# Modulation chunks multiplied in one visit of four instead of visits of one and two

## The chip, the cores and the metric
The kernel runs on one core of a Trainium2 chip. The metric is device time in microseconds of one execution; lower is better. PE is TensorE, PEld its weight loads, DVE is VectorE, ACT is ScalarE, POOL is GpSimd, SP is SyncE, which here issues the loads of weights.

## What is computed
Two model blocks one after the other on a sequence of 256 tokens of 2048 features, all in float32. The change lies in the first part of the first block: the modulation vector (one product of a 12288-column matrix, for two inputs `c` and `c_ctx`) and the input projection of `x` and of `ctx`.

```python
def adaln(cvec, w, b):
    m = jax.nn.silu(cvec) @ w + b
    return jnp.split(m[:, None, :], N_MOD, axis=-1)
...
        sh1, sc1, ga1, sh2, sc2, ga2 = adaln(c, w_mod[i], b_mod[i])
        csh1, csc1, cga1, csh2, csc2, cga2 = adaln(c_ctx[None, :], w_mod[i], b_mod[i])
        px = modulate(rms_norm(x, norm_mix[i]), sh1, sc1) @ w_in[i]
        pc = modulate(rms_norm(xc, norm_mix[i]), csh1, csc1) @ w_in[i]
...
        x = x + ga1 * yx
        x = x + ga2 * ffn(modulate(rms_norm(x, norm_ffn[i]), sh2, sc2),
                          w_gate[i], w_up[i], w_down[i])
```

`sh1` and `sc1` are needed for the projection. The other four parts (`ga1`, `sh2`, `sc2`, `ga2`) are needed much later, so their columns of `w_mod` are multiplied on the side, between the chunks of the projection.

## The kernel before
All weights stream from HBM in chunks of 512 rows by 256 columns (512 KB, `CK` = 4 blocks of 128 rows, `CN` = 256). A chunk is one DMA of SP into a buffer. `STREAM` (line 52) lists the phases in order: `mod` (shift and scale), then `in_kv`, `in_lora`, `in_r`, `in_rest` (the projection), `out`, `ffn` and so on. A phase has trips (loops), a trip has pairs (256 columns of output each, two PSUM banks), and a pair has four main chunks of rows, here called M0 to M3.

A **main chunk** is split into two parts, since a product of float32 precision is made from several faster ones: ACT copies its high part (`hi`, line 898), DVE subtracts to get the rest (`lo`, line 1330), and PE multiplies. `hi` and `lo` have four slots (`RING`); in `in_kv` and `in_lora` main chunks use only two of them, as the other two hold modulation chunks. In `in_kv` and the first pair of `in_lora` PE makes three products per block (lines 2127 to 2129, for `x` and `ctx`), in the second pair of `in_lora`, in `in_r` and in `in_rest` two (lines 2117 and 2118, `x` alone).

A **modulation chunk** (side chunk; `whole` in the code) is multiplied as it is, in `mod_rows` (line 2154): four matmuls of 32 columns of weights, each into its own quarter of a PSUM bank. Four modulation chunks make one side row of 256 columns. When the fourth is done, DVE copies the row out of PSUM (`mod_row2`, line 1464); PE turns it into columns with two small matmuls (`side_columns`, line 2220), which waits for that copy through `side_free` and stands behind the chunk that follows the row's last one; later DVE adds the bias (`mod_bias`, line 1469).

What fixes the order is `Phase.order`, written out in lines 72 to 81: a list of (side or main, pair or side row, rows) over one trip. Every engine walks this same list, in its own program order. With `SIDES` side rows a trip, two pairs a trip and four modulation chunks a row, `in_kv` and `in_lora` put two modulation chunks ahead of each main chunk, `in_r` and `in_rest` one. Trips and pairs: `in_kv` 4 trips of 2 pairs, `in_lora` 1 of 2, `in_r` 2 of 2, `in_rest` 4 of 2.

- **SP** (line 757) issues the loads in the order of the list; before each it waits for its buffer. A main chunk's buffer is free when its last content is split, a modulation chunk's when PE has used it; the first ones of the later buffers wait for a whole region, as `side_proj` does for the finished operand of the first layer (`region_free`, line 625).
- **ACT** (line 900) and **DVE** (line 1333): at entry j they first split all main chunks up to j + lookahead, then do the side work of this entry (`side`, such as the operand groups of `GROUP_AT` in `in_kv`, or the convolution and small vectors in `in_rest`), and then the evacuation of a pair or the copy of a side row that j completes. A split of `hi` waits until PE has used its slot before.
- **PE** (line 2081): at entry j it waits for the split or the load, multiplies, and then runs `after`, here the columns.

The lookahead (line 327) is 4 in `in_kv` and `in_lora`, 6 in `in_r` and `in_rest`.

The evacuation of a pair is on DVE: in `in_kv` four shifted multiply-adds on 128x510 (lines 1475 and 1477) behind two copies of ACT; in `in_r` ACT's copy (919), DVE's sum (1359), ACT's scaled copies (1020) and DVE's four multiply-adds; in `in_rest` ACT's copy and DVE's sum alone. In the third and fourth trip of `in_rest`, `conv`, `conv_gate` and `lam_powers` on DVE and `conv_and_rates` on ACT run behind certain entries of the list.

Of the kernel before, what the change touches and what calls it, by code (L numbers as in the profile page):

```python
# [63 lines left out]
class Phase:  # L64


    def __init__(self, name, trips, pairs, rows, g0, p0):
        self.name, self.trips, self.pairs, self.rows = name, trips, pairs, rows
        self.per_pair = n = rows // CK
        self.g0, self.p0 = g0, p0  # L70

        self.order = []
        if name == "out_2":
            self.order = [(False, p, c) for c in range(n) for p in range(pairs)]
        self.rows_order = (0, 2, 3, 1) if name == "out" else range(n)
        if name == "out":
            self.order = [(False, p, c) for cs in ((0, 2, 3), (1,)) for p in range(pairs) for c in cs]
        for p in range(pairs if name not in ("out", "out_2") else 0):
            for c in self.rows_order:
                per = SIDES.get(name, 0) // pairs  # L80
                self.order += [(True, per * p + t // n, t % n) for t in range(per * c, per * c + per)] + [(False, p, c)]
        self.chunks = len(self.order)

    def chunk(self, i, j):
# [165 lines left out]
def program(nc, A, out):  # L250
# [6 lines left out]
    def at(name, offset, shape, dt=F32):  # L257
        return nc.alloc_sbuf_tensor_at(name, shape, dt, offset=base + offset)
# [7 lines left out]
    mod = at("mod", fix + 2048, [P, 2, 6 * KB])  # L266
# [57 lines left out]
    bank_free, tmp_ready = sem("bank_free"), sem("tmp_ready")  # L324
    SPLIT_CREDIT, BANK_CREDIT = RING, 2
    EARLY = {"mod", "in_kv", "in_lora", "in_r", "in_rest"}
    lookahead = lambda ph: 2 if ph.name == "mod" else 4 if ph.name in ("in_kv", "in_lora") else 6 if ph.name in EARLY else 3
    SPLIT_EARLY = [PH["out"].chunk(0, 2), PH["out"].chunk(0, 3), PH["out"].chunk(0, 4), PH["out"].chunk(0, 5), PH["ffn"].chunk(0, 3)]
    TURN = (1, 3, 4, 6)
    VEC_AT = 5  # L330
# [2240 lines left out]
```

How the kernel before makes its waits and increments, by code:

```python
    def wait(self, eng, name, rounds=0):  # L146
        eng.wait_ge(self.sem, self.value(name, rounds))
# [13 lines left out]
    def wait(self, value):  # L161
        self.eng.wait_ge(self.sem, value)
# [536 lines left out]
    def load_vectors(eng, which):  # L699
        eng.wait_ge(vec_clear, 1)
        for number, (name, (t, first, n)) in enumerate(VROWS.items()):
            if number % 2 != which:
                continue
            if name.startswith("shift"):
                c0, width = {"shift_rkv": (0, P), "shift_gd": (GD0, P), "shift_wd": (WD0, LORA),
                             "shift_ad": (WD0 + LORA, LORA)}[name]
                src = A["rw_shift"][:, c0:c0 + n // 3 * width]
                for tap in range(3):
                    eng.dma_start(vrow[first + tap * (n // 3):first + (tap + 1) * (n // 3), t, 0:width],
                                  src[tap].rearrange("(n c) -> n c", c=width)).then_inc(vec_in[which], 16)
                continue
            src = A[name]
            names = " ".join("abcd"[:len(src.shape)])
            flat = src.rearrange(f"{names} -> ({names})") if len(src.shape) > 1 else src
            eng.dma_start(vrow[first:first + n, t, :], flat.rearrange("(n c) -> n c", c=P)).then_inc(vec_in[which], 16)
# [43 lines left out]
                def trip(i):  # L760
# [5 lines left out]
                            load_vectors(sp, 0)  # L766
                        if chunks[ph.chunk(i, j)].raw_free:
                            sp.wait_ge(*chunks[ph.chunk(i, j)].raw_free)
                        dst, arrives, _ = raw_at(ph, i, j)
```

## Time and profile before
| | |
|---|---|
| Median of three executions | 3071.35 us (3059.32 to 3072.09) |
| The profiled execution | 3060.31 us, span 3058.4 us |
| PE busy | 2976.7 us, 97% of the span |
| DVE busy | 1861.4 us, 61% |
| ACT busy | 1386.1 us, 45% |
| Mean granted clock of TensorE | 0.988 of full |
| Chain that ended last | PE 86%, DVE 8%, DMA 3% |

The phases that the change touches run from about 116 to 564 us. The page cuts the span in 40 slices and gives the busy share of each engine in tenths; in the slices from 153 to 562 us PE has a 9 in each. The busy time of PE counts matmuls that overlap, so a full share says that it had no hole, not that it worked at its peak; the timelines show by their start times what a step costs. A timeline row is: start, duration, engine, line, operation, output and inputs, shape, count of records merged, and in brackets the idle time before it with who ended it. A float32 matmul of `mod_rows` leaves two records.

### The profile page before, as it was taken

What the parts mean: (1) busy time and instruction counts of PE and PEld (TensorE: products, weight loads), DVE (VectorE), ACT (ScalarE), POOL (GpSimd) and SP (SyncE); (2) the same over time, 40 slices, a digit from 0 to 9 for tenths busy, and PEclk for the clock granted to TensorE, in tenths of its full rate; (3) what the DMA queues carried; (4) which work ended last, traced back from release to release, by engine and by line L of the source; (5) the groups of instructions that cost most, each with busy time, mean ns of one, the idle gap of its engine ahead of it and who ended that gap; (6) DMA issues with size and microseconds to landing.
All of it is one profiled execution on the core that took longest, in us unless ns stands there. A gap on an engine that the chain in (4) does not pass through costs nothing.

```text
span 3058.4 us, 62116 instructions
## 1 busy us (share of the span) xinstructions
PE 2976.7 (97%) x26987; PEld 2522.6 (82%) x26987; DVE 1861.4 (61%) x2655; ACT 1386.1 (45%) x1985; POOL 242.0 (8%) x299
## 2 busy tenths in 40 slices
PE   5899999999999999999999999999999999999998
PEld 2677777889888887888888888888888888888887
DVE  1333354677788776555555555789976666665554
ACT  1411233565665444444444444456644444444433
POOL 1000000143332200000000000012200000000000
PEclk7999999999999999999999999999999999999999
DMA  9997799200000065655666555655556666656664
GB/s 339 289 287 228 250 314 297 80 8 8 8 12 8 19 221 156 186 183 185 192 185 186 186 186 186 213 171 162 162 165 191 188 189 189 188 189 196 189 190 144
DMA packets 549240, 529.54 MB, mean 173 GB/s; under 512 B 16916, under 2 KB 545706, under 8 KB 548074
## 3 DMA queue, kind: packets, MB, share of 16 engines
q1 hardware_dynamic: 546074, 516.08, 54.0%
q0 software_dynamic: 2832, 9.49, 0.9%
q8 instruction: 214, 3.51, 0.5%
q14 instruction: 56, 0.46, 0.0%
q10 hardware_dynamic: 64, 0.02, 0.0%
HBM read 521.32 MB, written 4.19 MB: 172 GB/s over the span
## 4 chain that ended last, share of the span: by engine, by line
PE 86%; DVE 8%; DMA 3%; issue 1%; SPq 1%; ACT 1%; DVEq 0%; ACTq 0%
PE ps L2117 41%; PE ps L2118 20%; PE ps L2254 10%; PE ps L2158 2%; PE ps L2127 2%; DVE lo L1330 2%; PE ps L2128 2%; PE ps L2129 2%; DMA raw_more<-in_w_mod 1%; PE ps L2277 1%; PE ps L2264 1%; PE ps L2510 1%; PE ps L2262 1%; DVE dirs L1740 1%; SPq L773 1%
## 5 line engine op out<-in xcount | busy, mean ns | idle before, releaser
L1330 DVE TENSOR_TENSOR lo<-raw,hi 128x1024 fp32r<-128x1024 f32 x776 | 947.6, 1237 | 710.5 <-ACT hi L898 707.7
L2117 PE MATMUL ps<-mov,hi 128*128 128x512 f32 x3680 | 1299.3, 398 | 4.9 <-DVE mov L1393 4.1
L898 ACT ACTIVATE hi<-raw 128x1024 fp32r<-128x1024 f32 x776 | 810.7, 1056 | 864.8 <-PE ps L2118 652.3
L2118 PE MATMUL ps<-mov,lo 128*128 128x256 f32 x3680 | 1027.4, 279 | 0.0
L2117 PEld LDWEIGHTS ps<-mov,hi 128*128 128x128 f32 x3680 | 691.7, 188 | 191.6 <-issue 27.1
L2118 PEld LDWEIGHTS ps<-mov,lo 128*128 128x128 f32 x3680 | 694.0, 189 | 0.1
L2117 PE MATMUL ps<-hid,hi 128*128 128x512 f32 x704 | 248.8, 399 | 0.0
L919 ACT ACTIVATE tmp<-ps 128x512 f32<-128x512 f32 x157 | 93.8, 598 | 254.4 <-PE ps L2118 247.0
L2118 PE MATMUL ps<-hid,lo 128*128 128x256 f32 x704 | 197.7, 281 | 0.0
L2510 PE MATMUL ps<-mov,hi 128*128 128x512 f32 x512 | 187.1, 408 | 0.0
L812 POOL TENSOR_TENSOR lev<-U,kscan 128x256 f32<-128x256 f32 x192 | 152.1, 828 | 236.7 <-ACT U L1126 236.7
L2117 PEld LDWEIGHTS ps<-hid,hi 128*128 128x128 f32 x704 | 132.3, 188 | 33.2
L2117 PE MATMUL ps<-hid_2a,hi 128*128 128x512 f32 x448 | 155.7, 394 | 0.0
L2511 PE MATMUL ps<-mov,lo 128*128 128x256 f32 x512 | 142.7, 279 | 0.0
L2118 PEld LDWEIGHTS ps<-hid,lo 128*128 128x128 f32 x704 | 133.0, 189 | 0.0
L2118 PE MATMUL ps<-hid_2a,lo 128*128 128x256 f32 x448 | 124.1, 277 | 0.0
L2127 PE MATMUL ps<-mov,hi 128*128 128x512 f32 (+1 forms) x288 | 118.0, 410 | 2.9 <-DVE lo L1330 2.9
L2510 PEld LDWEIGHTS ps<-mov,hi 128*128 128x128 f32 x512 | 96.1, 188 | 23.1 <-DVE lo L1330 1.4
L2128 PE MATMUL ps<-mov,hi 128*128 128x512 f32 (+1 forms) x288 | 114.2, 396 | 0.0
L2129 PE MATMUL ps<-mov,lo 128*128 128x512 f32 (+1 forms) x288 | 113.3, 394 | 0.0
L2117 PEld LDWEIGHTS ps<-hid_2a,hi 128*128 128x128 f32 x448 | 84.0, 188 | 19.5
L2254 PE MATMUL ps<-dirs,lev 64*64 64x64 f32 x2560 | 91.7, 220 | 8.2 <-DVE dirs L1740 3.3
(387 smaller groups left out, 3841.4 us busy)
## 6 DMA issues: line engine op xcount, KB each, us to landing
raw<-in_w_in SPq DMA_DIRECT2D x184, 512.0 KB, 4.7
raw<-in_w_gate SPq DMA_DIRECT2D x88, 512.0 KB, 4.5
raw<-in_w_up SPq DMA_DIRECT2D x88, 512.0 KB, 4.5
raw<-in_w_down SPq DMA_DIRECT2D x88, 512.0 KB, 4.4
raw<-in_w_ffn_gate SPq DMA_DIRECT2D x88, 512.0 KB, 4.5
raw<-in_w_ffn_up SPq DMA_DIRECT2D x88, 512.0 KB, 4.6
raw<-in_w_ffn_down SPq DMA_DIRECT2D x88, 512.0 KB, 4.4
raw<-in_w_out SPq DMA_DIRECT2D x64, 512.0 KB, 4.5
```

The source lines that it names most:

```text
L812: scan_pool[d].done(pool.tensor_tensor(LEV[l][d][:, :, :], U[d][:, :, :], over_chunks(level[1 - d][l]), ALU.mult), (q, f"m{l}"))
L898: act.activation(hi[:, s, :, :], src, ACT.Copy).then_inc(hi_ready, 1)
L919: act.activation(tmp[:, t, :, :], ps[:, b:b + 2, T:2 * T], ACT.Copy).then_inc(tmp_ready, 1)
L1330: dve.tensor_tensor(lo[:, s, :, :], raw_at(ph, i, j)[0], hi[:, s, :, :].bitcast(F32), ALU.subtract)\
L2117: pe.matmul(ps[:, b, :], hi[:, s, kk, w], moving(k, None), start=first, stop=False)
L2118: mm = pe.matmul(ps[:, b, 0:T], lo[:, s, kk, w], moving(k, 0), start=False, stop=last)
L2127: pe.matmul(ps[0:widths, b, :], hi[:, s, kk, w], mov1[:, k, 0, :, :], start=first, stop=False)
L2128: pe.matmul(ps[0:widths, b, :], hi[:, s, kk, w], mov1[:, k, 1, :, :], start=False, stop=False)
L2129: mm = pe.matmul(ps[0:widths, b, :], lo[:, s, kk, w], mov1[:, k, 0, :, :], start=False, stop=last)
L2254: mm = pe.matmul(ps[hs, 4 * d + bank, off + c * n:off + (c + 1) * n], lhs(c, hs), moving, start=True, stop=True)
L2510: pe.matmul(ps[:, b, :], w_hi[:, kk, :], on_mov(k, None), start=(k == 0), stop=False)
L2511: mm = pe.matmul(ps[:, b, 0:T], w_lo[:, kk, :], on_mov(k, 0), start=False, stop=(k == KB - 1))
```

## The change
The list puts all four modulation chunks of a side row together, ahead of the main chunk where the row began: in `in_kv` and `in_lora` four ahead of M0 and four ahead of M2 of each pair, in `in_r` and `in_rest` four ahead of M0. The number of chunks and what is multiplied stay the same. The lookahead becomes 5 in all four phases (and stays 2 in `mod`, 3 in the later ones).

```diff
@@ -78,7 +78,8 @@
         for p in range(pairs if name not in ("out", "out_2") else 0):
             for c in self.rows_order:
                 per = SIDES.get(name, 0) // pairs
-                self.order += [(True, per * p + t // n, t % n) for t in range(per * c, per * c + per)] + [(False, p, c)]
+                side = c * per // n if per and c * per % n == 0 else None
+                self.order += [(True, per * p + side, t) for t in range(n) if side is not None] + [(False, p, c)]
         self.chunks = len(self.order)
 
     def chunk(self, i, j):
@@ -324,7 +325,7 @@
     bank_free, tmp_ready = sem("bank_free"), sem("tmp_ready")
     SPLIT_CREDIT, BANK_CREDIT = RING, 2
     EARLY = {"mod", "in_kv", "in_lora", "in_r", "in_rest"}
-    lookahead = lambda ph: 2 if ph.name == "mod" else 4 if ph.name in ("in_kv", "in_lora") else 6 if ph.name in EARLY else 3
+    lookahead = lambda ph: 2 if ph.name == "mod" else 5 if ph.name in EARLY else 3
```

One trip of `in_rest` (s a modulation chunk, M a main one; two pairs) is s M s M s M s M twice before, and ssss MMMM twice after. One pair of `in_kv` is ss M ss M ss M ss M before, and ssss M M ssss M M after.

## Rows read from the trace of the kernel before
**Rows 1.** Windows: the stretch of `in_r`, busy time, clock, DMA, GB/s.
```profile
core 0: us, PE busy (x) PEld busy (x) DVE busy (x) ACT busy (x) POOL busy (x), PEclk, DMA share, GB/s
372.00:462.00 90.00, 90.00 (x639) 67.07 (x637) 50.45 (x69) 35.39 (x43) 0.56 (x1) 1.00 0.98 311
```
**Rows 2.** Waits of PE from 130 to 600 us: total, times, longest.
```profile
PE ps L2254 <- ACT XY L1136: 1.0, 1, 1.0
```
**Rows 3.** Timeline of PE in `in_rest`, around one visit of one chunk.
```profile
461.89 0.50 PE L2220 MATMUL ps<-basics,mrow 128*128 128x2 f32 x4
...
465.70 0.28 PE L2118 MATMUL ps<-mov,lo 128*128 128x256 f32 x1
465.91 0.64 PE L2158 MATMUL ps<-side_ctx,c 128*32 128x256 f32 x8
466.48 0.50 PE L2117 MATMUL ps<-mov,hi 128*128 128x512 f32 x1
466.81 0.28 PE L2118 MATMUL ps<-mov,lo 128*128 128x256 f32 x1
466.93 0.40 PE L2117 MATMUL ps<-mov,hi 128*128 128x512 f32 x1
...
469.45 0.42 PE L2158 MATMUL ps<-side_ctx,c 128*32 128x256 f32 x4
```
**Rows 4.** Timeline of PE in `in_kv`: a main chunk and a visit of two.
```profile
167.05 0.50 PE L2127 MATMUL ps<-mov,hi 128*128 128x512 f32 x1
...
172.76 1.07 PE L2158 MATMUL ps<-side_r,c 128*32 128x256 f32 x16
173.76 0.50 PE L2127 MATMUL ps<-mov,hi 128*128 128x512 f32 x1
```
**Rows 5.** Timeline of PE in `in_r`: what follows a pair's last chunk.
```profile
403.46 0.50 PE L2220 MATMUL ps<-basics,mrow 128*128 128x2 f32 x4
```
**Rows 6.** Timeline of DVE in `in_r`, behind that pair's evacuation.
```profile
407.71 2.36 DVE L1330 TENSOR_TENSOR lo<-raw,hi 128x1024 fp32r<-128x1024 f32 x2
...
415.33 0.43 DVE L1464 COPY mrow<-ps 128x256 f32<-128x256 f32 x1 [1.75 <-PE ps L2158]
```
**Rows 7.** Timeline of DVE in `in_rest`: the first split behind an evacuation.
```profile
463.67 1.23 DVE L1330 TENSOR_TENSOR lo<-raw,hi 128x1024 fp32r<-128x1024 f32 x1 [0.26 <-ACT hi L898]
```
**Rows 8.** Timeline of DVE, third trip of `in_rest`: side work.
```profile
508.63 1.22 DVE L1546 TENSOR_TENSOR proj<-proj 128x1024 f32<-128x1024 f32 x1
...
519.27 0.47 DVE L1475 SCALAR_TENSOR_TENSOR ymix<-proj,vec,ymix 128x252 f32<-128x252 f32 x1
```
**Rows 9.** Timelines of ACT and DVE, fourth trip of `in_rest`: side work.
```profile
536.57 0.20 ACT L1030 ACTIVATE lcol<-vec 128x8 f32<-128x8 f32 x1
...
538.20 0.62 ACT L1033 ACTIVATE wdad<-wdad 96x512 f32<-96x512 f32 x1
...
541.41 0.17 DVE L1526 TENSOR_SCALAR lcol<-vec 128x8 f32<-128x8 f32 x1
...
542.13 0.42 DVE L1558 TENSOR_TENSOR ymix<-ymix,proj 128x256 f32<-128x256 f32 x1
```
**Rows 10.** Timeline of all engines in `in_lora`: pair's end, first split behind it.
```profile
372.04 0.50 PE L2220 MATMUL ps<-basics,mrow 128*128 128x2 f32 x4
...
375.96 1.21 DVE L1330 TENSOR_TENSOR lo<-raw,hi 128x1024 fp32r<-128x1024 f32 x1
```
**Rows 11.** Timelines of DVE, ACT and PE at the start of `in_kv`.
```profile
141.59 0.48 DVE L1450 SCALAR_TENSOR_TENSOR mov<-xhat_last,mod,mov 128x256 fp32r<-128x256 f32 x1
...
149.01 1.06 ACT L898 ACTIVATE hi<-raw 128x1024 fp32r<-128x1024 f32 x1 [8.18 <-DMA raw<-in_w_in]
...
153.32 0.50 PE L2127 MATMUL ps<-mov,hi 128*128 128x512 f32 x1
```
**Rows 12.** PE: a long wait in the timeline; windows of PE with the clock.
```profile
2214.94 0.55 PE L2481 MATMUL ps<-kret,p 128*128 128x128 f32 x1 [2.73 <-DVE p L2023]
...
1156.00:1166.00 10.00, 5.86 (x18) 0.51 0.03 12
...
2214.00:2221.00 7.00, 6.06 (x17) 0.52 0.43 141
```

## Prediction
> **What bounds the kernel now.** I read the granted clock and the busy shares by stretch first, then what PE waited for, then the timelines of PE, DVE and ACT around one modulation visit. In the stretch that the change touches, PE is busy for all of the 90.00 us from 372 to 462 at full clock, DVE for 50.45 and ACT for 35.39 [rows 1]; and from 130 to 600 us the longest wait of PE for anyone is 1.0 us [rows 2]. So PE sets the time there, DVE is behind it with slack, and two things count: what PE spends on visits, and whether the slack of DVE survives a new order. The sum is made against the profiled execution, 3060.31 us (span 3058.4), which lies 11 us below the median of 3071.35.
>
> **What goes: visits.** PE passes 88 times from main chunks to modulation chunks and back: `in_kv` 32 times, `in_lora` 8, `in_r` 16, `in_rest` 32. After it, 16, 4, 4 and 8, so 32; 56 visits go, no chunk does. A visit of one chunk: the last main matmul starts at 465.70, the next main one at 466.48, so 0.78; without a visit it is 0.12 (466.81 to 466.93), and the first main pair is longer by 0.10 after it (466.48 to 466.81 is 0.33, usually 0.23), so 0.76 [rows 3]. The eight records of one chunk take 0.57 to the next main matmul, the sixteen of two chunks 1.00 [rows 3, 4]: a chunk more costs 0.43. What is left, 0.76 - 0.43 = 0.33 us, is the price of the visit. 56 x 0.33 = **18.5 us gained**, all on the path. Bounds: 0, if a visit of four has a cost in it that I don't see (none is in the trace), and 0.45 a visit, 25 us.
>
> **What moves: the copy that PE waits for.** Line 1464 on DVE takes the finished side row out of PSUM; PE's next step on it, the columns of line 2220, stands one chunk later in PE's order, and PE works in order: all main chunks are queued behind it. Before, the modulation chunk that completes a row comes last in a pair, and that chunk and the main one behind it cover the copy. Now all four chunks come first, the columns are due right after the first main chunk M0, and DVE has in its order, between the end of the pair before and this copy: the evacuation of that pair, the splits of M1, M2 and M3 (with a lookahead of 5 they are called at j = 0, 1 and 2 of the pair, the copy at j = 3), any side work, then the copy. Let T be where PE begins what follows the last main chunk.
>
> PE after T: a visit of four, 0.57 + 3 x 0.43 = 1.86; then M0, 466.48 to 469.45 less the 0.09 by which the next visit starts later, 2.9. Columns are due at T + 4.8 in `in_r` and `in_rest` [rows 3].
>
> *After a pair of `in_r` or the second of `in_lora`*, T is 403.46 [rows 5]. DVE begins its first split behind the evacuation at 407.71, two of them take 2.36, so three 3.5, the copy 0.43 [rows 6]: done at 411.65, seen at 411.7, due at 408.3. **Gap 3.4 us**, five times (four pairs of `in_r`, the first of `in_rest`): 17.0.
>
> *After a pair of `in_rest`*, T is 461.89 [rows 3]; the first split starts at 463.67 [rows 7], copy done at 467.6, due at 466.7. **Gap 1.0**, three times: 3.0.
>
> *The last four pairs* carry side work ahead of the copy. Third trip: a product of 1.22 in the first pair, two blocks of two taps of 0.5 in the second [rows 8]: gaps 2.2 and 3.1. Fourth trip, first pair: ACT puts 2.25 us (536.57 to 538.82, a table load in it) between the hi parts of M2 and M3, and DVE a gate of 0.42 and 0.7 of small operations (541.41 to 542.13) [rows 9]: hi of M3 ends 6.0 after T, split 7.2, gate and small ones 8.3, copy 8.8, gap 4.0. Second pair: another such load, and the lookahead now reaches the first chunk of `out`, whose split (1.2) comes ahead of the copy: gap 4.3 likewise. Together 13.6.
>
> *`in_kv`* has longer main chunks, 5.7 from 167.05 to the next visit at 172.76 [rows 4]: due at T + 7.5, while DVE is through the evacuation at T + 3.9 and done with one split and the copy by T + 5.6 [rows 10]. No gap; the 1.9 us left are the cover. *`in_lora`*, second pair, short chunks: the same DVE work against T + 4.8: gap 0.8.
>
> Gaps: 17.0 + 3.0 + 13.6 + 0.8 = **34.4 us lost**. Bounds: 20, if one split fewer stood ahead of each copy than I order (five gaps of 2.2, the short ones none, 8.9 of the last four); 38, with semaphore and restart times of 0.3 more each.
>
> **The start of `in_kv`.** SP keeps its order: four modulation chunks now stand ahead of M0 and again ahead of M4. Today the operand of the first layer is ready at 142.07, which frees the buffers of the next modulation chunks; M4 is the third load behind that and lands by 149.01, its split is done at 151.3, PE needs it at 153.32: slack 2.0 [rows 11]. After it M0 lands two loads later (0.52 MB at the 311 GB/s of [rows 1] is 1.7 us each; the queue was not always full there, so I take 1.45), M1 ends near 139.7, and the call for M3's hi, which needs M1's end, moves from j = 7 to j = 6, ahead of the last two groups of the operand: hi until 140.8, then two times four steps of about 0.45 on ACT with DVE behind each, ready near 145.9, 3.9 us later. M4 is the fifth load, 2.9 later. 3.9 + 2.9 - 2.0 = **4.8 us lost** (bounds 1 and 8: the loads may overlap more, the start may be slower). Before M4 PE stands for 3.3 us, as the four modulation chunks ahead of it land in time to be done near 154.9. Further loads have more lead than now: with gaps a pair of `in_r` takes 17 us for the same eight chunks, and its DMA share of 0.98 [rows 1] falls.
>
> **The clock.** Where PE stood for 2.73 us, after a stretch at full clock, the granted clock was 0.52 over the next 7 us (2214 to 2221), the lower of its two levels, 1.2 of 2.4 GHz [rows 12]. Of such a time some 5.5 us are work behind a gap of 3.4, at half the clock: at most 2.75 lost, 2.5 taken. Nine gaps are of 2.7 us or more (the start, five, three of the last four): 9 x 2.5 = **22.5 us lost**. Bounds: nothing, and 3.9 each if the clock stays low for 10 us, as from 1156 to 1166 [rows 12].
>
> The Trainium skill, "TensorE: Matmul & The Clock Gate", section "HAM oscillation — how this bites in real kernels", says that a wait in every tile of a loop lets the clock fall in every tile, and gives a rule of thumb from what length on idle gaps hurt. The 2.73 us here lie under that length and the clock fell all the same, so the trace does not agree and I go by it; by the rule only the two gaps of over 4 us would pay, 5 us in place of 22.5, and the sum would be 3097.
>
> **Sum.** -18.5 + 34.4 + 4.8 + 22.5 = +43.2: 3060.3 + 43.2 = 3103.5 on the profiled execution, and 3071.35 + 43.2 = 3114.5 on the median, which I predict.
>
> **The rivals.**
> *The clock holds* through gaps of 3 to 4 us between bursts of 13 us: -18.5 + 34.4 + 4.8 = +20.7, so 3092 on the median (3081 on the profiled level). For it: the fall is seen behind one gap that stands alone. Against: the other low stretch, at 0.51, stands behind waits for DVE too [rows 12], and [rows 2] has no wait above 1.0 us that the clock outlived.
> *Gaps about half as long*, if a split stands elsewhere than I order it: 17 us of gaps, only the start and the table loads slow the clock (7.5 less 2.5 for a shorter start): -18.5 + 17 + 4.8 + 5 = +8, 3079. Against it: DVE's order is fixed in the program.
> *Faster*: the copy comes in time, because something shortens the DVE queue between T and M0's end from 8.2 us to 4.8; then only the visits count, -18.5, 3053. It decides at a copy done by T + 4.8; today's rows put its earliest finish there at T + 5.7, behind the short evacuation.
> *The change doesn't do what it says*: a visit of four costs as much as two of two. Then 18.5 more, 3133.
>
> **How the numbers follow.** Forecast with gaps and clock 0.55, clock holds 0.18, half gaps 0.13, faster 0.10, no saving 0.04. The forecast's own range is 3097 to 3134 (gaps 28 to 38, clock 1.5 to 3.5 each). Down to 3076 the range takes in the clock holding on either level of the median and the upper part of the half gaps; what is left out is the faster case, the low part of the half gaps and a tail above. Range 3076 to 3134. 0.5% is 15 us, about what can be told from no change here. Slower by more than that: 0.55 + 0.04 + 0.17 = 0.76; faster 0.10 with a few of its runs within 15 us, so 0.09; the rest, 0.15, within.
>
> **What would show it.** In the profile after: PE waits for DVE's copy of L1464 at the columns, some twelve times, 3.4 us after `in_r`; sixteen or thirty-two records of L2158 in a row; 56 fewer stretches in which a weight load of a main chunk waits for issue; a granted clock of half in several places between 380 and 600 us; a wait for M4's split near 155. Wrong it would be if PE's busy time stays closed from 372 to 564, or if the copy stands ahead of the splits.

## The result and the profile after
The kernel after takes 3109.93 us (median of four runs, 3088.86 to 3115.49) against 3065.34 for the kernel before (3059.12 to 3072.09) run beside it. The medians lie 44.6 us apart, the means of the four runs each 40.6 us, which is a ratio of 1.0132, with a 95% interval of 1.0077 to 1.0188. So the change makes the kernel slower, by some 40 to 45 us; a median of 3114.5 was predicted, with a range of 3076 to 3134. The profiled execution took 3111.11 us, span 3109.2, at a mean granted clock of 0.981.

From the edit of the list on, lines of the kernel after are one further down than before (L1465 is the copy, L2221 the columns, L2159 the modulation matmuls, L2118 and L2119 the products of `x` alone, L1331 `lo`).

Waits of PE in the kernel after, 110 to 620 us (total, times, longest), to be held against [rows 2]:
```profile
PE ps L2221 <- DVE mrow L1465: 30.8, 13, 4.0
PE ps L2128 <- DVE lo L1331: 3.3, 1, 3.3
```
Before, no wait of PE from 130 to 600 us was above 1.0 us. Now PE stands thirteen times at the columns for DVE's copy of the side row, and once for M4's split. Both kernels have one more wait ahead of 130 us, in front of M0 of `in_kv`: 2.9 us before, 2.8 after. Ahead of that lie waits for loads, of 1.5 us at most before and 1.9 after.

Where one of them comes from, in the first pair of `in_r`, behind the evacuation of `in_lora`: timelines of PE, then of DVE, in the kernel after:
```profile
398.11 0.61 PE L2221 MATMUL ps<-basics,mrow 128*128 128x2 f32 x4 [3.15 <-DVE mrow L1465]
...
393.64 0.48 DVE L1478 SCALAR_TENSOR_TENSOR gd<-px,vec,gd 128x255 f32<-128x255 f32 x1
...
394.24 3.49 DVE L1331 TENSOR_TENSOR lo<-raw,hi 128x1024 fp32r<-128x1024 f32 x3
397.64 0.42 DVE L1465 COPY mrow<-ps 128x256 f32<-128x256 f32 x1
```
DVE goes without a pause from the evacuation through the bias (0.16 us, left out here) and three splits (3.49 us) to the copy; it ends at 398.06 and PE starts at 398.11. The row itself was complete at 391.87, where PE began M0 behind the visit. The copy is late by its place in DVE's list.

Windows of the kernel after (PE busy, clock, DMA share, GB/s; the first also with PEld, DVE, ACT and POOL behind PE). The first answers to [rows 1]; the others lie behind six of the waits:
```profile
372.00:462.00 90.00, 76.81 (x526) 60.52 (x525) 39.32 (x56) 26.68 (x34) 0.56 (x1) 0.92 0.80 257
...
398.00:406.00 8.00, 7.89 (x37) 0.79 1.06 350
416.00:424.00 8.00, 7.25 (x25) 0.57 1.06 345
455.00:463.00 8.00, 7.39 (x43) 1.00 1.06 352
472.00:480.00 8.00, 7.17 (x43) 1.00 1.06 348
532.00:537.00 5.00, 4.52 (x18) 0.66 0.92 285
549.00:557.00 8.00, 6.28 (x21) 0.57 1.04 335
```
In the first stretch PE is busy for 76.81 us of 90 where it was busy for all of them; DVE's work fell from 50.45 to 39.32, as less of the program fits in the window (526 records of PE in place of 639). The clock is at half for a part of the time behind the waits at 398.11 and 416.75 (3.15 and 3.19 us in the timeline), but not behind those at 455.61 and 472.83, which are as long, 3.15 us each.

**Where the time went.** The starts of PE's first matmul of a phase or trip give a table by stretch. M0 is the first main chunk of a phase or trip; the columns run from M0 to M0, the last one from M0 to the last main matmul of `in_rest`. All numbers are in us, from one profile of each kernel; the experiments in it are told below.

| kernel | M0 of `in_kv` to M0 of `in_r` | `in_r` | `in_rest`, trips 1 and 2 | trip 3 | trip 4 |
|---|---|---|---|---|---|
| before | 266.84 | 58.48 | 58.42 | 29.22 | 28.09 |
| after | 267.60 | 74.73 | 60.80 | 36.93 | 38.90 |
| e_fill | 268.49 | 68.76 | 61.14 | 32.88 | 33.42 |
| e_la6 | 269.56 | 74.03 | 58.50 | 30.45 | 36.22 |
| e_late | 268.58 | 58.27 | 55.42 | 27.22 | 25.16 |
| e_late_groups | 262.33 | 58.03 | 55.76 | 27.23 | 25.15 |
| b_all | 262.45 | 55.31 | 54.45 | 27.23 | 26.05 |
| e_kv_clean | 267.08 | 58.44 | 58.43 | 29.21 | 28.10 |
| b_rest_clean | 268.05 | 54.98 | 54.45 | 27.23 | 25.99 |

After is 37.9 us longer than before over these five stretches; `in_r` gives 16.3 of it, the last two trips 18.5. The borders move a little with the order: one modulation chunk more lies in the first column of after (0.43) and three fewer in the last (1.3). From the first visit of `in_kv` (116.87 before, 114.90 after) to the first wait of the next phase (578.13, 616.93) the kernel after takes 40.8 us longer; this is the figure for the terms of the prediction to be held against.

The two profiled spans differ by 50.8 us. Some 13 us of that come after 2200 us, where the change touches nothing. One group of matmuls of the last stage, in the kernel before, then in the kernel after (form, count, busy us, mean ns of one, idle time before them):
```profile
L2117 PE MATMUL ps<-hid_2b,hi 128*128 128x512 f32 x256 | 89.1, 394 | 0.0
...
L2118 PE MATMUL ps<-hid_2b,hi 128*128 128x512 f32 x256 | 90.8, 399 | 0.0
```
The same matmuls, with no wait, go 1.9% slower in the one execution (90.8 for 89.1). It isn't the change's doing: among the kernels below, all with the same code there, the mean is 391, 394 or 399 ns, and `e_late`, `e_la6` and `e_fill`, which have the new order throughout, show 394 like the kernel before. The medians, which are over several executions, differ by 44.6.

### The profile page after: what moved, and what is told of

Read it like the earlier page. It is cut to its first block, busy times and chain, and to the rows that moved or that the text cites. A ratio compares the mean times of both kernels' runs of the same rounds, so it can differ in the third digit from the quotient of the medians.

```text
span 3109.2 us, 62114 instructions
## 1 busy us (share of the span) xinstructions
PE 2994.7 (96%) x26987; PEld 2547.5 (82%) x26987; DVE 1859.2 (60%) x2655; ACT 1382.0 (44%) x1985; POOL 241.9 (8%) x299
## 4 chain that ended last, share of the span: by engine, by line
PE 84%; DVE 10%; DMA 3%; ACT 2%; issue 1%; SPq 1%; DVEq 0%; ACTq 0%
PE ps L2118 40%; PE ps L2119 20%; PE ps L2255 10%; DVE lo L1331 4%; PE ps L2128 2%; PE ps L2129 2%; PE ps L2130 2%; DMA raw_more<-in_w_mod 2%; PE ps L2159 1%; PE ps L2278 1%; PE ps L2265 1%; PE ps L2511 1%; PE ps L2263 1%; DVE dirs L1741 1%; PE ps L2221 1%
## 5 line engine op out<-in xcount | busy, mean ns | idle before, releaser
L1331 DVE TENSOR_TENSOR lo<-raw,hi 128x1024 fp32r<-128x1024 f32 x776 | 946.4, 1237 | 700.3 <-ACT hi L899 698.1
L2118 PE MATMUL ps<-mov,hi 128*128 128x512 f32 x3680 | 1318.2, 403 | 4.8 <-DVE mov L1394 4.1
L2119 PE MATMUL ps<-mov,lo 128*128 128x256 f32 x3680 | 1038.9, 282 | 0.0
L2118 PEld LDWEIGHTS ps<-mov,hi 128*128 128x128 f32 x3680 | 699.9, 190 | 183.3 <-issue 6.2
L2119 PEld LDWEIGHTS ps<-mov,lo 128*128 128x128 f32 x3680 | 703.0, 191 | 0.1
L2118 PE MATMUL ps<-hid,hi 128*128 128x512 f32 x704 | 248.8, 399 | 0.0
L2119 PE MATMUL ps<-hid,lo 128*128 128x256 f32 x704 | 197.7, 281 | 0.0
L2511 PE MATMUL ps<-mov,hi 128*128 128x512 f32 x512 | 187.2, 408 | 0.0
L2118 PEld LDWEIGHTS ps<-hid,hi 128*128 128x128 f32 x704 | 132.3, 188 | 33.0
L2118 PE MATMUL ps<-hid_2a,hi 128*128 128x512 f32 x448 | 158.7, 399 | 0.0
L2119 PEld LDWEIGHTS ps<-hid,lo 128*128 128x128 f32 x704 | 133.0, 189 | 0.0
L2119 PE MATMUL ps<-hid_2a,lo 128*128 128x256 f32 x448 | 125.8, 281 | 0.0
L2511 PEld LDWEIGHTS ps<-mov,hi 128*128 128x128 f32 x512 | 96.1, 188 | 23.0 <-DVE lo L1331 1.2
L2118 PEld LDWEIGHTS ps<-hid_2a,hi 128*128 128x128 f32 x448 | 84.2, 188 | 21.0
```

What stands on the lines that cost most here:

```text
L1331: dve.tensor_tensor(lo[:, s, :, :], raw_at(ph, i, j)[0], hi[:, s, :, :].bitcast(F32), ALU.subtract)\
L2118: pe.matmul(ps[:, b, :], hi[:, s, kk, w], moving(k, None), start=first, stop=False)
L2119: mm = pe.matmul(ps[:, b, 0:T], lo[:, s, kk, w], moving(k, 0), start=False, stop=last)
L2511: pe.matmul(ps[:, b, :], w_hi[:, kk, :], on_mov(k, None), start=(k == 0), stop=False)
```

## The experiments
Each kernel is the one after with the edit shown; the ratio is to the kernel before, run on the same chip in the same job, with its 95% interval. The kernel before had medians of 3060.89, 3060.74 and 3061.55 us in the three jobs; a ratio takes in all runs of a job, so it can differ by some tenths of a per cent from that of the medians.

**Columns later (e_late).** If the copy costs time only because PE needs it so early, a later step of PE takes the cost away. In `in_r` and `in_rest` PE's columns go from one entry behind a row's last chunk to three; the order of DVE's work stays.
```diff
-                    done = ph.completed(j - 1) if j else None
+                    late = 3 if ph.name in ("in_r", "in_rest") else 1
+                    done = ph.completed(j - late) if j >= late else None
```


> The changed kernel, with one edit: in in_r and in_rest PE makes the columns of a side row three entries of the list after the row's last chunk (behind M2) instead of one (behind M0). DVE's order is untouched. My theory (PE stands because it reaches the columns before DVE's copy, which is queued behind three splits): the waits of PE for the copy go from 30.8 us to about 0.5 (the one of in_lora), in their place PE may wait some 0.6 us for M1's split in five pairs; the clock stays at full from 380 to 600; what is left is 18.5 us gained by visits against 3 to 5 us lost at the start of in_kv, so about 3052 to 3062, 0.2 to 0.4% below the kernel before. Rival (the visits of four themselves or the splits' place cost the time, the wait only shows it): the time stays near 3100, and the wait turns up at the splits instead.


Measured: 3053.51 us, 0.9974 (0.9946 to 1.0003). Waits of PE, 110 to 620 us:
```profile
PE ps L2128 <- DVE lo L1331: 3.3, 1, 3.3
PE ps L2118 <- DVE lo L1331: 2.7, 5, 0.6
```
The waits for the copy are gone but for one of 0.6, no low clock is left from 380 to 600 us (the window shows 1.00), and the five stretches take 434.7 where after takes 479.0. So the time lost lies in where PE waits for the copy and in what follows from that. What is left is five short waits for splits (0.5 to 0.6 us each, where the lookahead of 5 is now a little short) and the start of `in_kv`.

**A lookahead of 6 again (e_la6).** With the new order the lookahead decides what stands ahead of the copy. One entry more puts a split ahead of the evacuation in place of behind it.
```diff
-    lookahead = lambda ph: 2 if ph.name == "mod" else 5 if ph.name in EARLY else 3
+    lookahead = lambda ph: 2 if ph.name == "mod" else 5 if ph.name in ("in_kv", "in_lora") else 6 if ph.name in EARLY else 3
```
The last trip of `in_rest` keeps 5 (the loop over the lookahead is one shorter there).


> The changed kernel with the lookahead of in_r and in_rest back at 6, except in the last trip of in_rest, where it stays 5. So one split fewer stands ahead of each copy in DVE's queue. My theory: each of the five large gaps falls by one split, 3.15 to about 2.0 us, the three of 0.7 vanish, two of the last four fall by 1.2 and one by 0.9: waits of PE for the copy 30.8 to some 19 us, fewer falls of the clock, 3085 to 3100 in all. Rival (the lookahead of 5 is the whole cause and the new order costs nothing): the waits vanish and the time is below the kernel before, near 3050.


Measured: 3081.77 us, 1.0076 (1.0048 to 1.0105).
```profile
PE ps L2222 <- DVE mrow L1466: 20.8, 10, 3.9
```
The waits fall by 10.0 us, nearly as far as expected; the time lies a little below what was expected (3085 to 3100). The gaps do depend on the splits in the list, and the rival, in which the lookahead was the whole cause, falls: the time doesn't come down to 3050. But `in_r` hardly gains (74.73 to 74.03). Windows of PE from 380 to 470 us, in the kernel after, then in e_la6:
```profile
380.00:470.00 90.00, 77.05 (x528) 0.92 0.78 249
...
380.00:470.00 90.00, 80.26 (x530) 0.89 0.85 272
```
PE stands less there (five waits of 9.7 us in all, where after has four of 12.6), and the clock is low for longer. Three of the five are of 2.0 us now, and so is the next one behind them, at 475.51. Each of the four had half clock behind it: the windows from 421, 438 and 475, 6 us each, show 0.72, the one of 7 us from 456 shows 0.52. Shorter gaps didn't bring less of the low clock.

**The gaps filled (e_fill).** This separates the price of the clock from that of the gaps: ahead of its wait PE makes matmuls whose result nobody reads, about as many as fit in each gap.
```diff
+            def FILL(ph, i, m):
+                if ph.name == "in_r" or (ph.name, i, m) == ("in_rest", 0, 0):
+                    return 13
+                if ph.name == "in_rest":
+                    return (2, 2, 2, 2, 8, 11, 15, 17)[2 * i + m]
+                return 0
...
                         m = done[1]
+                        for n in range(FILL(ph, i, m)):
+                            pe.matmul(ps[:, 7, :], mov1[:, 0, 0, 1, 0:P], mov1[:, 0, :, 1, :], start=True, stop=True)
```


> The changed kernel, and PE multiplies something useless into a free bank ahead of each wait for the copy in in_r and in_rest: 13 matmuls of 512 columns at the large gaps (about 3.0 us), 2 at the small ones, 8 to 17 at the last four. Nothing else differs; the output doesn't use it. This tells the wait from the clock. My theory (a gap of about 3 us costs its own length and in more than half of the cases another 1.5 to 3 us of a clock at half): the waits for the copy fall to a few us in all, the time of the gaps stays, the granted clock is 1.00 from 380 to 600 us, and the time falls by 10 to 20 us against the changed kernel, to about 3090 to 3098. Rival (the clock costs nothing, as DVE and not PE sets the pace there): the time stays within 4 us of the changed kernel, 3106 to 3112.


Measured: 3084.63 us, 1.0072 (1.0043 to 1.0101). Windows of e_fill over two stretches of the kernel after that are shown above:
```profile
416.00:424.00 8.00, 7.78 (x46) 1.00 1.05 349
...
549.00:557.00 8.00, 8.00 (x68) 1.00 0.72 232
```
The useful work behind each gap starts no sooner after it than in the kernel after, and yet this is faster, by more than was expected (3090 to 3098): the clock is at 1.00 in both stretches, and over the whole of 380 to 600 us. Of the two ratios, 1.0072 here and 1.0132 for after, the intervals overlap, so it is the profile that shows the gain and not the times alone. From `in_r` on the table gives 196.2 us for 211.4, so 15.2 came back, and the clock is what differs. What after lost to the clock there is more than this, as the filling is a little longer than the gaps. The next section takes it from after itself.

**The two halves (e_kv_only, e_rest_only).** The new order in `in_kv` and `in_lora` alone, and in `in_r` and `in_rest` alone; the phases named in the edit keep the old list and the old lookahead.
```diff
+                if name in ("in_r", "in_rest"):
+                    self.order += [(True, per * p + t // n, t % n) for t in range(per * c, per * c + per)] + [(False, p, c)]
+                    continue
                 side = c * per // n if per and c * per % n == 0 else None
```


> The new order in in_kv and in_lora alone (lookahead 5 there); in_r and in_rest as before (order and lookahead 6). My theory: 20 visits go (-6.6 us), the start costs 3 to 5 us of waiting for M4's split and some 1.5 of low clock, in_lora 0.6: between -2 and +1 us against the kernel before, same; no wait of PE for the copy but 0.55 in in_lora. Rival (the start of in_kv carries much of the loss): 10 us or more slower than before.


Measured: 3066.97 us, 1.0031 (1.0005 to 1.0057).


> The new order in in_r and in_rest alone (lookahead 5 there); in_kv and in_lora as before (order and lookahead 4). My theory: 36 visits go (-11.9 us), the waits of PE for the copy stay, 30.2 us without that of in_lora, and the clock falls in several of them (10 to 17 us): 28 to 36 us slower than before, so nearly all of the changed kernel's loss. Rival (the loss is spread over all four phases): 10 to 20 us slower.


Measured: 3088.25 us, 1.0109 (1.0051 to 1.0167). The loss lies in `in_r` and `in_rest`, where the pairs are short; `in_kv` and `in_lora` have little of it. By the medians the second half is 27.5 us slower than the kernel before, just under the 28 to 36 that I expected. The first half came out worse than I expected, 6 us slower by the medians, and its timelines show why (DVE, then PE):
```profile
390.55 1.23 DVE L1334 TENSOR_TENSOR lo<-raw,hi 128x1024 fp32r<-128x1024 f32 x1 [3.65 <-ACT hi L902]
...
391.76 0.42 DVE L1468 COPY mrow<-ps 128x256 f32<-128x256 f32 x1
...
392.23 0.49 PE L2224 MATMUL ps<-basics,mrow 128*128 128x2 f32 x3 [2.87 <-DVE mrow L1468]
```
The lookahead of 5 in `in_lora` reaches over the end of the phase to the first main chunk of `in_r`, which there, with the old list, is only one chunk further. DVE waited 3.65 us for that chunk's `hi`, split it, and only then made the copy. That wait is of my edit, not of the change. The second half has one like it: with a lookahead of 4 in `in_lora`, `in_r`'s M0 is split behind the evacuation, and PE waits 3.3 us for it; it takes the place of the wait for the copy in that pair.

**The first half without that (e_kv_clean).** At two entries near the end of `in_lora`, 20 and 21 of 0 to 23, the lookahead stops short of `in_r`'s first main chunk:
```diff
-                        for n in range(1, lookahead(ph) + 1):
+                        for n in range(1, (24 - j if ph.name == "in_lora" and j in (20, 21) else lookahead(ph)) + 1):
```


> Visits of four in in_kv and in_lora alone, and the split of in_r's first main chunk kept behind the last copy of in_lora, so that the wait of 2.9 us of the run before it goes. Theory (a visit is worth 0.28 us, the start costs 5.7, the clock's fall near 157 us some 3): 20 visits x 0.28 = 5.6 gained, 5.7 + 0.7 + 3 lost, so about 4 us slower than before, ratio near 1.001, one wait for the copy of about 0.6 us and one for M4's split of 3.3. Rival (a visit is worth 0.33 and more and the start is hidden): 7 us faster, ratio 0.998.


Measured: 3062.41 us, 0.9996 (0.9972 to 1.0020); waits of PE:
```profile
PE ps L2131 <- DVE lo L1334: 3.3, 1, 3.3
...
PE ps L2224 <- DVE mrow L1468: 0.5, 1, 0.5
```
The waits are the two that were expected. The interval takes in both the theory's ratio (1.001) and the rival's (0.998), so the time doesn't tell them apart; the profile does. From the first visit of `in_kv` to M0 of `in_r` it takes 276.43 us (116.62 to 393.05) where the kernel before takes 272.94 (116.87 to 389.81), 3.5 longer, against some 4 of the theory. The 20 visits saved here don't quite pay for the start.

**The start of `in_kv` (e_late_groups).** e_late, with the last four groups of the operand made one or two entries earlier, so that the buffers come free earlier:
```diff
-    GROUP_AT = {0: 2, 1: 3, 3: 4, 4: 5, 6: 6, 7: 7}
+    GROUP_AT = {0: 2, 1: 3, 2: 4, 3: 5, 4: 6, 5: 7}
```


> The kernel with late columns, and the operand groups of the first layer called at j = 0 to 5 of in_kv instead of at 0, 1, 3, 4, 6 and 7, so that the last two stand ahead of M3's split. My theory of the start (M4's load is held up since the buffers ahead of it wait for the operand, which stands behind M3's split): the operand is ready near 137 instead of 145, the wait of PE for M4's split (3.3 us) vanishes with the fall of the clock behind it; 4 to 6 us less than with late columns alone. Rival (M4 is late because the queue of loads is full): the wait stays, no change.


Measured: 3050.97 us, 0.9961 (0.9929 to 0.9993). M4's wait is gone, and the first stretch takes 262.33 us for e_late's 268.58: 6.25 less, a little over what was expected. The medians, of two jobs, differ by 2.5 us only, and the intervals of the ratios overlap, so the times don't show this gain apart. PE in e_late, then in e_late_groups, in the windows and the timeline around M4:
```profile
154.00:168.00 14.00, 10.35 (x54) 0.76 1.10 351
...
155.45 1.93 PE L2159 MATMUL ps<-side_proj,c 128*32 128x256 f32 x32
157.31 0.50 PE L2128 MATMUL ps<-mov,hi 128*128 128x512 f32 x1
```
Of the 6.25 us 3.3 are the wait itself; the rest is the clock, which in e_late is at half for about half of the 14 us from 154 (0.76), and at 1.00 in that window in e_late_groups. The groups are all that was moved, so M4's wait came from the time at which the operand was finished, as the prediction put it. No run keeps a lookahead of 4 in `in_kv` with the new order, so how much of the start comes from the lookahead of 5 and how much from the list isn't shown.

**The faster version (b_all, b_rest_late, b_rest_clean).** b_all puts the three cures together: columns later, lookahead 6 in `in_r` and `in_rest`, groups earlier. b_rest_late leaves the old order in `in_kv` and `in_lora` and has columns later and lookahead 6. b_rest_clean is that with a lookahead of 5 at the last entry of `in_lora`.


> Late columns, lookahead 6 in in_r and in_rest, and the operand groups at j = 0 to 5, all with the new order in all four phases. My theory: no wait of PE for copy, split or load from 130 to 560 us but 0.6 in in_lora; only the 56 visits are left, so 15 to 19 us below the kernel before, ratio 0.994 to 0.995. Rival (something else in the new order costs PE time, or a visit costs less than 0.33 us): less than 10 us below.

> The new order in in_r and in_rest alone, with late columns and lookahead 6; in_kv and in_lora as before, with their old start. 36 visits go and no wait comes: my theory says 11 to 12 us below the kernel before, ratio 0.996. Rival (a visit costs half of what I read from the start times): 6 us below.

> Visits of four in in_r and in_rest alone, columns three entries later, lookahead 6 there, and the first main chunk of in_r split ahead of in_lora's evacuation. Theory: 36 visits x 0.28 = 10 us gained and nothing lost, since the wait of 3.3 us at 399 is gone and with it the fall of the clock behind it: ratio near 0.9967, from the first visit to the end of the projections 10 us less than before. Rival (the wait at 399 is not from the order of that split): it stays, and the ratio stays at 0.9986.


Measured: b_all 3035.57 us, 0.9942 (0.9915 to 0.9969); b_rest_late 3048.67, 0.9986 (0.9952 to 1.0020); b_rest_clean 3048.98 in a later job, 0.9954 (0.9927 to 0.9981). Waits of PE in b_rest_late for M0 of `in_r` and for the copy, then in b_rest_clean for M0:
```profile
PE ps L2121 <- DVE lo L1334: 3.3, 1, 3.3
...
PE ps L2225 <- DVE mrow L1468: 2.7, 2, 2.1
...
PE ps L2121 <- DVE lo L1334: 0.2, 1, 0.2
```
The wait for M0 went with the place of one split, as the theory had it and the rival not. It wasn't the only one in b_rest_late, which missed its expectation of no wait and 0.996: in `in_kv`, where this kernel has the old order, a load landed late (ACT stood 10.35 us for it, until 151.97; 8.18 us, until 149.01, in the kernel before), and PE waited 2.1 us for the copy that stands behind that chunk's split. From M0 of `in_kv` to M0 of `in_r` b_rest_late takes 275.05 us and b_rest_clean 268.05; the two waits and 3.4 us of half clock behind the first, which cost half of that, make up the 7.0. So the step from 0.9986 to 0.9954 is in part that load, and the two intervals overlap. b_all has two waits for the copy of 0.6 us and one for a split of 0.6 from 130 to 560 us, two more than expected. b_all and b_rest_clean are both faster than the kernel before, and by about what the visits are worth (b_all's ratio is 18 us, with 9.5 to 26 in its interval): the order of the change is good for about half a per cent once the copy has its time. b_all has the lowest median of all kernels here, though its interval overlaps those of b_rest_clean, e_late_groups and e_late.

## Why the prediction was right, point by point
**The visits.** Trip 3 of `in_rest` holds eight modulation chunks between its M0 and the next in both orders, and six visits fewer in the new one; without waits it takes 27.22 us in e_late (508.19 to 535.41) and 29.22 before:
```profile
506.71 0.50 PE L2117 MATMUL ps<-mov,hi 128*128 128x512 f32 x1
...
535.93 0.50 PE L2117 MATMUL ps<-mov,hi 128*128 128x512 f32 x1
```
2.0 / 6 = 0.33 us a visit, the predicted figure. A visit of four takes 1.87 in the kernel after (464.73 to 466.60), 1.86 predicted. In `in_kv`, between its first chunk and `in_lora`'s, 16 visits fewer give 4.7 us in e_late_groups, 0.29 each. So the 56 visits are worth 17 to 18 us, 18.5 predicted, and they were gained; the rival in which the change doesn't do what it says falls.

**The gaps at the copy.** Predicted 34.4 us, in thirteen places by the prediction's own list ("some twelve" in its last paragraph). Measured 30.8 in thirteen, and 0.16 more from each end of a wait to the pace of before (restart), about 33 in all. There are four of 3.15 to 3.19 in `in_r`'s pairs and one more of 3.15 in the first of `in_rest` (3.4 predicted), three of 0.66 to 0.73 in the next pairs (1.0); the last four are 2.03, 2.74, 3.55 and 3.98 (2.2, 3.1, 4.0, 4.3), and the one in `in_lora` is 0.55 (0.8). Each is 0.2 to 0.5 shorter than predicted. In the first pair of `in_r`, with T at 390.01, the copy ended 8.05 us after T and not 8.2, and PE's M0 ended 4.96 after it and not 4.8. The rival of gaps half as long falls: the order of DVE's list held, three splits ahead of the copy. So does the faster case: its point was a copy done by T + 4.8.

**The start of `in_kv`.** Predicted 4.8, with PE standing 3.3 ahead of M4. The wait is 3.30 us. M0 starts 9.4 us after the first visit of `in_kv` and not 6.1; 0.9 of the difference is two more modulation chunks, which later places lack, 2.4 is M0's load. Together, with 0.16 for the restart, 5.9, inside the bounds of 1 and 8. The prediction took it as the delay of M4 as a whole. Counted so, from the first visit, M4 starts after 42.6 us (157.46) and not after 36.4 (153.32): 6.1 later. Less the 0.9 of the two chunks, plus the 0.6 that two visits fewer gave back by then, this is 5.8, next to the 5.9. ACT and DVE in the kernel after:
```profile
144.44 0.48 DVE L1451 SCALAR_TENSOR_TENSOR mov<-xhat_last,mod,mov 128x256 fp32r<-128x256 f32 x1
...
155.01 1.06 ACT L899 ACTIVATE hi<-raw 128x1024 fp32r<-128x1024 f32 x1 [10.60 <-DMA raw<-in_w_in]
```
The operand was ready at 144.9, 1.0 sooner than predicted; ACT then waited for M4's load until 155.0.

**The clock.** Predicted nine falls of 2.5 us, 22.5. In `in_r` the stretch grew by 16.25 us: 12 visits less (4.0), four gaps with their restarts more (12.64 + 0.64), which leaves 6.9 for the clock. The same sum gives 0.5 in the first two trips of `in_rest`, 4.6 in the third, 6.3 in the fourth: 18.3 in all. It agrees with the clock itself: over 399 to 598 us it was at half for 37.5 us in seven pieces of 3.4 or 6.8 us, and half of that is 18.7. At the start it was at half for 3.4 us more (0.72 in the window from 156 to 162), at most 1.7. So eight falls cost 20 us, 2.5 each on average, where nine of 2.5 were forecast. That this term came so near is in part luck. Which gaps the falls followed was not as predicted: two of the five of 3.15 to 3.19 brought no fall, and the one of 2.03 at 532.48 did. And no fall cost 2.5: those of 3.4 us cost 1.7 and those of 6.8 cost 3.4, and there were four of each. The rival in which the clock holds was wrong for seven of the nine gaps; e_fill shows the price apart, 15 us back with the clock at full.

The Trainium skill, "TensorE: Matmul & The Clock Gate", section "HAM oscillation — how this bites in real kernels", gives an idle time above which gaps hurt; the prediction went against it on the strength of one wait of 2.73 us. The trace of after doesn't agree with it as a threshold either: the clock fell behind waits of 2.03 and 2.74 us, below it. What that section says of a loop, that each tile that waits starts at the low clock again, agrees in the main: three falls in the four pairs of `in_r`.

**The sum.** -17.5 for the visits, +33 for the gaps, +5.9 for the start, +20 for the clock: +41. The profiles have 40.8 from the first visit of `in_kv` to the first wait behind `in_rest`. Predicted was +43.2, measured by the medians +44.6, by the means +40.6 and by the profiled spans +50.8, of which 13 are the slower matmuls behind 2200 us. The four runs of the kernel after spread over 27 us, so that its median came within 5 us of the forecast is luck too. The terms that were off are small and of both signs: the gaps 1 too large, the start 1 too small, the clock 2.5 too large, the visits 1 too large. The predicted level of the profiled execution (3103.5) was 8 below what was measured, within those 13.

The Trainium skill, "PSUM — Partial Sum Buffer", section "Engine vs sequencer instructions", states that the queues of ScalarE, VectorE and GpSimd are strictly first in, first out. The DVE rows of after agree: the copy at 397.64 followed three splits although its row had been complete since 391.87, and in e_kv_only a copy stood behind a split that itself waited 3.65 us for ACT.

**Open.** It stays open why two waits of 3.15 us, at 455.61 and 472.83, left the clock alone and three of 3.15 to 3.19 us didn't. The other profiles show that neither the length nor the place alone decides it. In e_la6 all eight waits of 2.0 to 3.9 us behind 130 us had half clock behind them, four of them of 2.0; in e_rest_only seven of nine of 2.0 to 3.9 us had, and one of 3.16 (at 435.30) had not. The wait on which the prediction built its term stands in all kernels, in code that the change leaves alone. Windows behind it, in after (a wait of 2.92 us) and in e_fill (2.89 us):
```profile
2253.00:2260.00 7.00, 7.00 (x30) 0.76 0.44 141
...
2239.00:2246.00 7.00, 6.42 (x34) 1.00 0.45 143
```
In the kernel before it was 2.73 us long and the clock around its end 0.52 [rows 12]. So one row of one profile couldn't tell what each gap would cost, and another execution of the same kernel may have another number of falls. Nor do the runs show why some executions multiply 1 or 2% slower through a whole stage.

## What to carry to other kernels
A change of order that saves an engine's switches also moves the copies that this engine waits for; write out, for the engine that makes the copy, everything between the end of the step before and the copy, and hold it against the work that the waiting engine has left. Here 17.5 us of switches were paid for with 33 us of gaps and 20 of clock. With the waiting step two entries later the same order had no long gap left there and was no slower than the kernel before (0.9974), and with the two other cures it was 0.6% faster. If a lookahead is counted in entries of a list, a new list changes what it reaches, over the end of a phase above all: three of the experiments had a wait of about 3 us from that alone.

## What the runs showed of the hardware that was not expected
- In the kernel after, behind 130 us, a wait of PE of 2 to 4 us in a full stretch brought the granted clock down to half in eight of ten cases, for 3.4 or 6.8 us, and not in the two of 3.15 us named above; the cost was half of the low time (18.3 us on the path for 37.5 us at half). The same wait of 2.7 to 2.9 us was followed by a clock of 0.52, 0.76 or 1.00 over 7 us in three kernels with the same code there.
- Useless matmuls in the gaps kept the clock at 1.00 from 380 to 600 us and made the stretches from `in_r` on 15.2 us shorter (196.2 for 211.4), though the gaps stayed as long.
- The change between the full 128x128 form of a matmul and the 128x32 one and back costs 0.33 us where the main matmuls are of the two-product kind (2.0 us for six, over a trip in which neither kernel waits), and 0.29 where they are of the three-product kind (4.7 us for 16).
- The same matmuls without a wait took 391, 394 or 399 ns in different executions, at a granted clock of 1.00.
